# Key norms in a decoder trunk: one product, a root on ScalarE and a reciprocal on VectorE in place of a small power on GpSimd

## The reference, cut to what matters

```python
kk = hd(k * k_k)                                   # (token, head, 64)
kk = kk / jnp.maximum(jnp.linalg.norm(kk, axis=-1, keepdims=True), 1e-12)
k  = k * (1 + (a - 1) * k_a)
b_h = kk * a_h
# the recurrence over tokens, per head
sa = einsum('bhvk,bhk->bhv', state, -kk_t)
state = state * w_t + sa[..., None] * b_t + v_t[..., None] * k_t
y_t = einsum('bhvk,bhk->bhv', state, r_t)
# y is then centred and scaled per head, a bonus is added, a gate multiplied
```

## Time and profile before

| | us |
|---|---|
| median of the runs | 1127.74 |
| the profiled execution, its own time | 1124.39 |
| its span, first to last instruction | 1122.3 |
| PE busy | 1086.0 (97%) |
| DVE busy | 811.9 (72%) |
| ACT busy | 567.2 (51%) |
| POOL busy | 53.5 (5%) |

### The profile page before, as it was taken

How to read it: one execution, slowest core, us unless ns; L and a number is a source line. 1 busy time by engine, 2 the same in 40 slices (tenths; PEclk the granted TensorE clock), 3 DMA queues, 4 the chain that set the end, 5 groups by cost and what they waited for, 6 DMA issues and landing times. The chain is left out here.

```text
span 1122.3 us, 31849 instructions
## 1 busy us (share of the span) xinstructions
PE 1086.0 (97%) x13568; PEld 986.0 (88%) x13568; DVE 811.9 (72%) x1483; ACT 567.2 (51%) x992; POOL 53.5 (5%) x49
## 2 busy tenths in 40 slices
PE   8999999999999899999999999999999999999996
PEld 8888888888898899998898888888889979999985
DVE  2678787868586887784557887979686768777745
ACT  3644555645444565553246445556454445555531
POOL 0000000000000100000010000000000010000000
PEclk9999999999999999999999999999999999999998
DMA  8533132222475566666463333222225736666661
GB/s 297 169 100 119 60 105 77 88 79 88 138 253 172 169 198 189 191 187 206 148 227 133 132 87 93 79 89 88 81 74 190 227 129 208 205 188 188 208 187 57
DMA packets 45525, 165.58 MB, mean 148 GB/s; under 512 B 5168, under 2 KB 5424, under 8 KB 45136
## 3 DMA queue, kind: packets, MB, share of 16 engines
q1 hardware_dynamic: 42736, 154.03, 42.8%
q0 software_dynamic: 1504, 7.47, 2.3%
q10 hardware_dynamic: 1152, 2.10, 0.6%
HBM read 160.44 MB, written 3.15 MB: 146 GB/s over the span
## 5 line engine op out<-in xcount | busy, mean ns | idle before, releaser
L750 PE MATMUL ps<-x_tok_r,mid_hi 128*128 128x256 f32 x576 | 175.8, 305 | 0.5 <-DVE ring_r L1702 0.5
L752 PE MATMUL ps<-x_tok_r,ring_r 128*128 128x256 f32 x576 | 162.2, 282 | 0.0
L751 PE MATMUL ps<-yb_hi,mid_hi 128*128 128x256 f32 x576 | 162.2, 282 | 0.0
L750 PEld LDWEIGHTS ps<-x_tok_r,mid_hi 128*128 128x128 f32 x576 | 108.7, 189 | 9.0 <-issue 1.4
L1702 DVE TENSOR_TENSOR ring_r<-ring,mid_hi 128x1024 fp32r<-128x1024 f32 x80 | 96.9, 1211 | 19.9 <-ACT mid_hi L1297 19.8
L751 PEld LDWEIGHTS ps<-yb_hi,mid_hi 128*128 128x128 f32 x576 | 109.0, 189 | 0.7 <-issue 0.7
L1297 ACT CAST mid_hi<-ring 128x1024 fp32r<-128x1024 f32 x80 | 83.8, 1047 | 50.6 <-PE ps L752 41.3
L752 PEld LDWEIGHTS ps<-x_tok_r,ring_r 128*128 128x128 f32 x576 | 108.9, 189 | 0.0
L1955 DVE TENSOR_TENSOR rs_ks_r<-ring,tha_kkn_r 128x1024 fp32r<-128x1024 f32 x44 | 53.9, 1224 | 21.8 <-ACT tha_kkn_r L1349 21.8
L1955 DVE TENSOR_TENSOR w_lo<-ring,w_hi 128x1024 fp32r<-128x1024 f32 x42 | 51.4, 1224 | 22.2 <-ACT w_hi L1349 22.1
L1955 DVE TENSOR_TENSOR vs_dC_r<-ring,b_k_r 128x1024 fp32r<-128x1024 f32 x44 | 53.7, 1221 | 17.4 <-ACT b_k_r L1349 17.4
(11 more groups left out here) (485 smaller groups left out, 3331.4 us busy)
## 6 DMA issues: line engine op xcount, KB each, us to landing
ring<-stream_dram SPq DMA_DIRECT2D x281, 512.0 KB, 3.8
lora_w<-lora_dram POOLq DMA_DIRECT2D x2, 1536.0 KB, 7.6
W_bt<-rpar_dram POOLq DMA_DIRECT2D x4, 512.0 KB, 5.2
kt_V<-rpar_dram POOLq DMA_DIRECT2D x4, 512.0 KB, 7.2
x_tok<-x_dram SPq DMA_DIRECT2D x2, 512.0 KB, 4.8
v_saved_dram<-vs_dC ACTq DMA_DIRECT2D x4, 256.0 KB, 4.4
x_tok<-x_dram SPq DMA_DIRECT2D x1, 1024.0 KB, 6.1
vf<-v_saved_dram ACTq DMA_DIRECT2D x4, 256.0 KB, 3.6
```

The lines of the kernel that those rows point to most:

```text
L750: pe.matmul(dst, lh, rh, start=start, stop=False)
L751: pe.matmul(dst, lh, rl, start=False, stop=False)
L752: return pe.matmul(dst, ll, rh, start=False, stop=stop)
```

## The change: what it does

In each of the eight rounds the sums of squares come from one product with `bones` (a 128 x 128 matrix of ones within each head) as the weights and `tmp`, 512 columns, moving. The result is already spread over the features. VectorE clamps the whole 128 x 512 tile into `kkn`, ScalarE takes the square root in place, VectorE the reciprocal in place, and the key product reads `kkn` in place of PSUM. The transpose, the spreading products, VectorE's small copy and the power on GpSimd go. Besides, three pieces of VectorE's order move: the scaled keys come behind chunk 1's state instead of ahead of it, `y_center` moves to the end of its own round, and the row maximum of the attention (`att_max`, without its masking part) moves behind the first half of level 2.

```diff
-        pe_prep ... + ["rnT", "rnx"]
+        pe_prep ...
-        pool_prep = by_round("pool_prep", ["rn"])
+        act_norm = by_round("act_norm", ["norm"])
 (TensorE)
-                for b in range(GB):
-                    for t in range(TT):
-                        j = 2 * (TT * b + t)
-                        mm = pe.matmul(bank(4)[:, j:j + 2], tmp[:, b, t * P:t * P + P], C["hsel"], start=True, stop=True)
-                mm.then_inc(*pe_prep.inc(r, "ss"))
-            def prep_rnT(r): ...
-            def prep_rnx(r): ...
+                pe.matmul(bank(4), C["bones"], flat(tmp), start=True, stop=True).then_inc(*pe_prep.inc(r, "ss"))
 (ScalarE)
+            def key_norm(r):
+                act.wait_ge(*dve_prep(r, "ss"))
+                act.activation(flat(kkn), flat(kkn), ACT.Sqrt).then_inc(*act_norm.inc(r, "norm"))
                 prep_exp(r0)
+                key_norm(r0)
                 gate(l, 0)
...
+                        if c == 1 and nxt:
+                            key_norm(r + 1)
 (VectorE)
-                dve.tensor_scalar(ssm[:, :], bank(4)[:, 0:8], 1e-24, None, ALU.max).then_inc(*dve_prep.inc(r, "ss"))
+                dve.tensor_scalar(flat(kkn), bank(4), 1e-24, None, ALU.max).then_inc(*dve_prep.inc(r, "ss"))
             def prep_keys(r):
-                dve.wait_ge(*pe_prep(r, "rnx"))
+                dve.wait_ge(*act_norm(r, "norm"))
+                dve.reciprocal(flat(kkn), flat(kkn)).then_inc(*dve_prep.inc(r, "rcp"))
+                dve.wait_ge(*dve_prep(r, "rcp"))
                 for b in range(GB):
                     last = dve.scalar_tensor_tensor(out=kkn[:, b, :], in0=ks[:, b, :], scalar=cp(l, "k_k", GB * g + b),
-                                                    in1=tok(4)[:, b, :], op0=ALU.mult, op1=ALU.mult)
+                                                    in1=kkn[:, b, :], op0=ALU.mult, op1=ALU.mult)
...
-                            if nxt and c == 1:
-                                prep_keys(r + 1)
...
                         if c < NCH - 1:
                             chunk_s(r, c)
+                        if nxt and c == 1:
+                            prep_keys(r + 1)
+                            prep_keys_scaled(r + 1)
...
                     y_sum(r)
                     if nxt:
                         prep_bonus(r + 1)
+                        y_center(r)
```

More of the change, by code:

```diff
@@ L538, in trunk @@
         dve_prep = Steps(sem("dve_prep"), [(["ss"] if r % GROUPS else []) + ["s", "cum", "cp"]
-                                           + (["rnT", "pend"] if r % GROUPS else ["pend", "ss", "rnT"]) + [ "kkn", "k2", "kb", "arc", "bneg", "kp"]
+                                           + (["pend"] if r % GROUPS else ["pend", "ss"]) + ["rcp", "kkn", "k2", "kb", "arc", "bneg", "kp"]
                                            + (["v1", "v2", "v"] if r >= GROUPS else []) + ["rkk"] for r in range(R)])
-        pool_prep = by_round("pool_prep", ["rn"])
+        act_norm = by_round("act_norm", ["norm"])
         pe_wkv = by_round("pe_wkv", ["gramB", "gramK", "V", "tokB"]
@@ L831, in prep_ss @@
                 pe.wait_ge(*act_prep(r, "kk2"))
-                for b in range(GB):
-                    for t in range(TT):
-                        j = 2 * (TT * b + t)
-                        mm = pe.matmul(bank(4)[:, j:j + 2], tmp[:, b, t * P:t * P + P], C["hsel"], start=True, stop=True)
-                mm.then_inc(*pe_prep.inc(r, "ss"))
-            def prep_rnT(r):
-                pe.wait_ge(*pool_prep(r, "rn"))
-                pe.transpose(bank(4)[0:8, 128:256], rn[:, :], ident).then_inc(*pe_prep.inc(r, "rnT"))
-            def prep_rnx(r):
-                pe.wait_ge(*dve_prep(r, "rnT"))
-                for b in range(GB):
-                    for t in range(TT):
-                        j = TT * b + t
-                        mm = pe.matmul(tok(4)[:, b, t * P:t * P + P], C["rowsel"][0:8, j * P:j * P + P], rnT[:, :],
-                                       start=True, stop=True)
-                mm.then_inc(*pe_prep.inc(r, "rnx"))
+                pe.matmul(bank(4), C["bones"], flat(tmp), start=True, stop=True).then_inc(*pe_prep.inc(r, "ss"))
             def y_back(r):
@@ L1081, in wkv @@
                     mm.then_inc(*pe_wkv.inc(r, f"y{c}"))
-                    if g + 1 < GROUPS and c == 0:
-                        prep_rnx(r + 1)
                     fill(16 + 3 * c)
@@ L1201, in _ @@
                 first = sum([pair_pieces(l, ("gate", i), xT) for i in range(GATES_FIRST)], [])
-                for k, ps_ in enumerate(([], [prep_1], [prep_ss, prep_v], [prep_rnT], [prep_rnx])):
+                for k, ps_ in enumerate(([], [prep_1], [prep_ss, prep_v])):
                     for p in ps_:
@@ L1206, in _ @@
                         piece()
-                for piece in first[10:]:
+                for piece in first[6:]:
                     piece()
@@ L1852, in level @@
                             y_var(r - 1)
+                        if lev == 2 and k == 0:
+                            att_max(*divmod(r, GROUPS))
                     else:
@@ L1928, in att_masked, with att_masked_0 @@
                 masked_logits(l, g, 1).then_inc(*dve_att.inc(l, f"lh{g}"))
+            def att_masked_0(l, g):
+                masked_logits(l, g, 0).then_inc(*dve_att.inc(l, f"lg{g}"))
             def att_max(l, g):
-                masked_logits(l, g, 0).then_inc(*dve_att.inc(l, f"lg{g}"))
                 dve.wait_ge(*dve_att(l, f"lg{g}"))
@@ L2237, in topk @@
                     for i in range(TOPK // 8):
-                        if i == 5 and halfway:
-                            halfway()
                         dve.wait_ge(*dve_att(l, f"causal{t}" if i == 0 else f"rep{t}{i - 1}"))
@@ L2268, in _ @@
                 prep_ss(r0)
-                topk(1, lambda: prep_rn(r0))
+                topk(1)
                 prep_keys(r0)
+                prep_keys_scaled(r0)
                 prep_arc(r0)
@@ L2280, in _ @@
                         prep_bonus(r)
-                    if g:
-                        y_center(r - 1)
                     for lev in range(LEVELS):
@@ L2317, in _ @@
                                     rkv(l, g + 1, i % 3)
-                            if nxt and c == 1:
-                                prep_keys(r + 1)
-                            elif nxt and c == 2:
+                            if nxt and c == 2:
                                 prep_arc(r + 1)
                                 prep_bk(r + 1)
-                            elif nxt:
+                            elif nxt and c > 2:
                                 prep_v(r + 1)
@@ L2326, in _ @@
                             mids_up_to(l, mids_by(GAPS * g + 13))
-                        if nxt and c == 0:
-                            prep_rn(r + 1)
                         if c < NCH - 1:
                             chunk_s(r, c)
+                        if nxt and c == 1:
+                            prep_keys(r + 1)
+                            prep_keys_scaled(r + 1)
                         if c in (1, 2):
```

19 lines of the change are left out of this document (4 added, 15 removed).

## The result

The changed kernel takes 1164.46 us (median of 4 runs, 1162.06 to 1166.12), the kernel before 1126.50 beside it (4 runs, 1125.07 to 1127.91): 1.0337 times as long, 95% interval 1.0319 to 1.0354. The forecast was 1148 with 1136 to 1161. The direction was right and the time lies outside the range, 16.5 us above the forecast. The profiled execution took 1164.81 us, its span is 1163.0 and the mean granted clock 0.979 (before: span 1122.3, clock 0.991).

A forecast was written before the change was run, and what follows sets the result against it. TensorE, busy 97% of the span, was taken as the bound. Middle rounds 16.5 plus first rounds 6.3 less moves 2.5 gave 20.3 us; on 1124.4 that is 1144.7, plus 3.3 for the median: 1148, 80% range 1136 to 1161.

The forecast's parts named there:

- plus or minus 4 us in the range, none in the sum: Clock falls in the levels, 1.3 us each: which rounds are hit may change, so 4 us in the range only.
- the new wait of nearly 4 us a round could bring a fall of its own: Rival: clock falls in TensorE's new waits, about 1.3 us in each of eight, 10 us more, 1158; chance 0.07.
- The reciprocal: VectorE's 128 x 512 reciprocal, R: taken at 3.05 us from the row of four columns, range 0.43 to 4.4.
- 4.3 us as an estimate: Rival of eight passes a column at 0.96 GHz for the reciprocal: 4.3 us, time 1158; chance 0.15.
- The sum without the clock: All rounds together: 16.5 + 6.3 - 2.5 = 20.3 us slower, with no clock falls in it.
- R - 0.3: Loss per middle round at `Zs` of chunk 2, R being the reciprocal's time: 2.75 us, 16.5 over six rounds.
- The first rounds: First round of each layer: grams 3.1 us later in layer 0, whole 3.25 us paid in layer 1; together 6.3.
- The moves: Moves in VectorE's order save TensorE's waits in the levels: 0.5 us for five rounds, 2.5 in all, between 0 and 4.
- The new wait for `S` in chunk 1: TensorE's wait for the state in chunk 2 goes, and a new one of about 0.7 us comes in chunk 1.
- The cheap reciprocal: Rival: the reciprocal takes only 0.43 us, so the time is 1127; chance 0.13.
- the faster kernel: Rival: reciprocal at its lower bound and VectorE ahead, 15 us off, about 1113, part of it possible; chance 0.07.
- ScalarE on the path: Rival: a 1.38 us drain per table load makes the root late, 1.4 us more in six rounds, 1156; chance 0.04.
- TensorE's own work: Transpose and spreading products go: gross 1.3 us less per round, 10 in all, of which 0.45 a round is left.

The follow-up runs named there:

- e3: Changed kernel with products that nothing reads added on TensorE in the new waits of all eight rounds: 1146.86 us, ratio 1.0193.
- e10: Changed kernel with added products that nothing reads on TensorE in the six middle rounds only: 1153.23 us, ratio 1.0236.
- e5: Changed kernel with the reciprocal over 256 columns only, the other 256 multiplied by a constant: 1144.2 us, ratio 1.0164.
- e4: Kernel before with the three moves of VectorE's order alone, norms as before: 1124.5 us, ratio 0.9993.
- e11: Kernel before with two of the three moves (`y_center`, `att_max`), the keys where they were: 1125.8 us, ratio 0.9994.
- e6: Changed kernel with the three moves of VectorE's order undone: 1172.61 us, ratio 1.0413.
- e1: Changed kernel with the reciprocal replaced by a multiplication by a constant: 1124.99 us, ratio 0.9998.
- e2: Changed kernel with ScalarE's square root replaced by a plain copy that needs no table load: 1160.81 us, ratio 1.0316.
- e15: Kernel of e13 with `y_center` back in the next round for layer 1 alone: 1122.79 us (12 runs), ratio 0.9959.
- e13: As e8, but ScalarE's cast ahead of the norm, arc in chunk 3, layer 1's values behind `yt`: 1124.9 us, ratio 0.9995.
- e14: Changed kernel with the reciprocal in two halves, later keys' work, bias operand and layer 1's values behind `yt`: 1142.19 us, ratio 1.0133.
- e7: Changed kernel with root and reciprocal both made on ScalarE as exp(-0.5 ln s): 1140.87 us, ratio 1.0124.
- e8: As e7, with VectorE's keys, scaled keys and arc one chunk later: 1131.26 us, ratio 1.0038.

## Why the prediction was wrong

**The step that failed** is the clock's: "plus or minus 4 us in the range, none in the sum", with "the new wait of nearly 4 us a round could bring a fall of its own" as a rival at 0.07. The wait itself was forecast well (3.8 us in a middle round, 4.06 measured; about 4.3 in layer 0's first round, 4.63 measured). The clock fell at all eight. e3 prices the falls of the changed kernel at 16 to 17.6 us, but three of its eleven are in the levels, where the kernel before has four. By the prediction's own 1.3 us each, those four are some 5 us that e3 gives back too. So of the 38 us some 12 are the clock's and some 25 the lateness's, where the forecast had 0 and 20.3; this split is an estimate from medians and traces. The rival was the right mechanism and was priced a little low, at 8 x 1.3 = 10 us: a fall costs 1.2 to 2.4 us between chunks 2 and 3, 9.3 for the six, and more in the first rounds (e10: 6.4 for two). A fall in the levels can cost more than 1.3 as well: chunk 3 of the second round to the next takes 38.6 us with the `issue` wait of 1.6 and a fall, against 34.9 in e3 with neither. The forecast had computed the idle time and had seen that the clock falls in this kernel; the two should have been put together as the likeliest case, not as a rival.

**The reciprocal** was the forecast's largest term and had the right kind of size: 3.05 us taken, 3.35 measured. The row of the eight instructions, in ns (minimum, median, maximum):

```profile
L1747 DVE RECIPROCAL tha_kkn<-tha_kkn x8: 3344/3346/3348, 89.2 to 834.2; 128x512 f32<-128x512 f32 x8
```

With e5's 1745 ns for 256 columns a column costs (3346 - 1745)/256 = 6.25 ns, where the slope from four columns gave 5.7. The Trainium skill (VectorE: DVE Perf Modes, the walkthrough of the 8-slice pipeline) speaks of a repeat count of 8, from which the prediction made 4.3 us as an estimate. The trace does not agree with that estimate: 6.25 ns are six periods of the page's 0.96 GHz, not eight.

**The sum without the clock** met its number by luck. 20.3 us were forecast and e3 has 20.4, but by terms that cancel. The middle rounds lost more than R - 0.3: chunk 0 to 2 takes 3.21 us more in layer 0 (12.28 to 15.49, rounds of the earlier trace rows's kind) and about 3.6 in layer 1; in e3 the six lose 19.7 together, where the forecast had 16.5. Of these 3.2 us, 1.8 are the reciprocal's 0.30 us times six; why layer 1 loses more wasn't tried. The moves' 2.5 us weren't found (below). Against that, e3 has no fall in the levels, where the kernel before has four, some 5 us that the sum left in.

**The first rounds**: 3.1 and 3.25 us forecast, 3.7 and 5.5 found in the changed kernel with their falls. In layer 0 the grams begin at 97.42 where they began at 93.87, 3.55 us later, 0.28 of it already there when the search ends; the fall behind them stands in the place of the one that the kernel before has in this round's levels.

```profile
97.42 0.33 PE L878 MATMUL ps<-arc,b_k 64*64 64x128 f32 x2 [4.63 <-DVE b_k L1773]
```

In layer 1 e3, which has no fall, loses 2.9 of the 5.5. So the prediction's step (the whole reciprocal is paid there) holds, and the excess in layer 1 is the clock's.

**The moves**: 2.5 us were credited; e4 and e11 find 0.8 and 0.7 with an interval across zero. The new wait for `S` in chunk 1 came as forecast, 0.78 us. The move of the keys counted for little in the prediction (it saves a wait for `S` of up to 0.6 us a round), but by e6 the three moves are worth 8 us with a long reciprocal, and its waits point at this one: in the old place TensorE waits 5.2 us for `S` in place of 4.1 for `Zs`. The move of the keys alone wasn't run.

**The rivals.** The cheap reciprocal and the faster kernel fall with the 3.35 us row. e1 shows that the first was priced well: 1127 forecast, 1125.0 measured with an instruction of 0.42 us. "Faster" at an almost free reciprocal is refuted by the same run. ScalarE on the path falls by e2, and its drain of 1.38 us behind a table load (the Trainium skill, ScalarE: Activation LUTs) isn't in the trace: the root starts 0.01 us behind the end of the load (136.49 + 1.28 against 137.78).

**TensorE's own work**: that of the gross 1.3 us a round 0.45 is left was a fair reading for this order. With nothing of the norm ahead of `Zs`, e15 has 3.5 us in all, not the gross 10, and even these can be the missing falls in the levels. What is left on the way there wasn't taken apart.

Three things stay open. Why the clock fell at eight of twelve waits of 2.4 to 2.6 us and not at the others wasn't tried. Nor was what sets the falls in the levels, four in the kernel before and none in e1 and e3. And e15's gain over e13 is 2 us, too near to the spread of the runs to be put down to `y_center` alone.

## What to carry to other kernels

Price an instruction that comes into a nearly full engine's feed by where it stands, not by its length: the same 3.35 us cost 38 us, 20 with the clock held up, and 16 in two halves over two chunks with the seam in order (e14). They cost nothing where ScalarE made the function in time that it had idle (e13). Where the trace of before shows that the clock falls, and the sum says that TensorE will idle for several microseconds, put the fall into the sum, times the number of waits. And take a long element-wise function (here a reciprocal at 6.25 ns a column) apart from the engine that feeds TensorE, then look at what it now stands ahead of on the engine that received it.

## What the runs showed of the hardware

- VectorE's reciprocal of fp32 takes 3.346 us for 128x512 and 1.745 for 128x256, against 0.42 for a multiplication by a constant of 128x512.
- The granted clock went to 0.50 at 8 of 8 waits of 4.1 to 4.6 us (changed kernel), at 8 of 12 of 2.4 to 2.6 us in the middle rounds of e5 and e7 together, and at none of the `Zs` waits of 1.1 to 1.4 us (e1, e8). One fall came behind a wait of 1.6 us (changed kernel, 219.72). The same piece of TensorE's work between chunks 2 and 3 then took 7.3 to 8.4 us where it takes 6.02.
- With products that nobody reads, issued in the eight waits, no trace row in the rounds showed a granted clock under 1.00, and 16 to 17.6 us came back (e3).
- On ScalarE a function of another table costs its load, 1.283 us, and nothing more that the rows show. Ln and Exp took a load each.
